# Hybrid two-layer decoder trunk on one core: the last feed-forward slabs regrouped into a fifth pair of seven block products, and the end of each feed-forward phase reordered

## The reference

```python
D_MODEL, SEQ, D_FF, DEPTH = 1024, 512, 2816, 2
DEEPNORM_ALPHA = (2 * DEPTH) ** 0.25
FFN_RES_WEIGHT = 0.5

def swiglu(x, w1, w3, w2):
    return (jax.nn.silu(x @ w1) * (x @ w3)) @ w2

h = swiglu(x, ffn_w1[l, k], ffn_w3[l, k], ffn_w2[l, k])
x = layer_norm(DEEPNORM_ALPHA * x + FFN_RES_WEIGHT * h, ln_g[l, i], ln_b[l, i])
```

## Time and profile before

| what | value |
|---|---|
| median of 3 runs | 1949.17 us (1949.12 to 1950.05) |
| the profiled execution, its own time | 1950.58 us |
| span of its profile | 1948.8 us |
| PE busy | 1928.0 us, 99% of the span, 10793 matmuls |
| DVE, ACT, POOL busy | 1084.5, 633.4, 898.8 us (56, 32, 46%) |
| TensorE clock granted | 0.998 of full over the span |
| DMA | 185.45 MB, mean 95 GB/s |
| chain of work that ended last | PE 97%, DVE 2%, DMA 1% |

### The profile page before, as it was taken

How to read it: one execution, slowest core, us unless ns; L and a number is a source line. 1 busy time by engine, 2 the same in 40 slices (tenths; PEclk the granted TensorE clock), 3 DMA queues, 4 the chain that set the end, 5 groups by cost and what they waited for, 6 DMA issues and landing times.

```text
span 1948.8 us, 26135 instructions
## 1 busy us (share of the span) xinstructions
PE 1928.0 (99%) x10793; PEld 1633.9 (84%) x10793; DVE 1084.5 (56%) x1620; ACT 633.4 (32%) x789; POOL 898.8 (46%) x596
## 2 busy tenths in 40 slices
PE   8999999999999999999999999999999999999997
PEld 8888888978788888888988888889988988888886
DVE  2755473555373665653465647265544675546655
ACT  3333232264423233322333323232233123323321
POOL 4453555533324455445445446444433345355544
PEclk9999999999999999999999999999999999999999
DMA  6232322321204333232423232322222222332321
GB/s 235 92 106 87 130 87 87 106 74 66 66 23 152 109 107 108 65 108 87 152 87 108 65 129 87 108 87 88 69 84 66 66 77 97 108 128 89 108 66 44
DMA packets 135590, 185.45 MB, mean 95 GB/s; under 512 B 3360, under 2 KB 119088, under 8 KB 135472
## 3 DMA queue, kind: packets, MB, share of 16 engines
q1 hardware_dynamic: 135312, 183.53, 28.5%
q10 hardware_dynamic: 160, 0.26, 0.1%
HBM read 181.42 MB, written 2.10 MB: 94 GB/s over the span
## 4 chain that ended last, share of the span: by engine, by line
PE 97%; DVE 2%; DMA 1%; ACT 0%; issue 0%; SPq 0%; POOL 0%; DVEq 0%; ACTq 0%
PE psum L1506 31%; PE psum L1507 30%; PE psum L1508 30%; PE psum L1816 2%; PE psum L1757 1%; PE psum L1530 1%; PE psum L1789 1%; PE psum L1770 1%; DMA raw<-in_ffn_w 1%; PE psum L1844 0%; PE psum L1847 0%; PE psum L1834 0%; DVE xt_lo L1015 0%; DVE arena L1212 0%; ACT w_hi L757 0%
## 5 line engine op out<-in xcount | busy, mean ns | idle before, releaser
L694 POOL TENSOR_TENSOR w_lo<-raw,w_hi 128x512 fp32r<-128x512 f32 x524 | 848.8, 1652 | 922.4 <-ACT w_hi L757 897.8
L1506 PE MATMUL psum<-xt_hi,w_hi 128*128 128x512 f32 (+1 forms) x1824 | 675.0, 370 | 2.2 <-DVE w_lo L1372 0.9
L1507 PE MATMUL psum<-xt_lo,w_hi 128*128 128x512 f32 (+1 forms) x1824 | 670.8, 368 | 0.0
L1508 PE MATMUL psum<-xt_hi,w_lo 128*128 128x512 f32 (+1 forms) x1824 | 670.7, 368 | 0.0
L1506 PEld LDWEIGHTS psum<-xt_hi,w_hi 128*128 128x128 f32 x1824 | 343.8, 188 | 65.3 <-issue 4.5
L1508 PEld LDWEIGHTS psum<-xt_hi,w_lo 128*128 128x128 f32 x1824 | 343.8, 189 | 57.1
L1507 PEld LDWEIGHTS psum<-xt_lo,w_hi 128*128 128x128 f32 x1824 | 343.9, 189 | 55.9
L757 ACT ACTIVATE w_hi<-raw 128x2048 fp32r<-128x2048 f32 x132 | 251.7, 1911 | 345.4 <-PE psum L1508 343.5
L1076 DVE SCALAR_TENSOR_TENSOR x<-psum,x 128x512 f32<-128x512 f32 x224 | 145.6, 684 | 131.5 <-PE psum L1508 128.3
L771 ACT ACTIVATE gate<-psum 128x512 f32<-128x512 f32 x88 | 52.5, 598 | 307.9 <-PE psum L1508 307.9
L1506 PE MATMUL psum<-w_hi,xt_hi 128*128 128x256 f32 (+2 forms) x448 | 139.8, 312 | 0.0
(11 more groups left out here) (178 smaller groups left out, 2147.1 us busy)
## 6 DMA issues: line engine op xcount, KB each, us to landing
raw<-in_ffn_w SPq DMA_DIRECT2D x115, 1024.0 KB, 5.4
raw_odd<-in_ffn_w SPq DMA_DIRECT2D x16, 1024.0 KB, 5.1
raw<-in_hgrn_w_in SPq DMA_DIRECT2D x16, 1024.0 KB, 5.5
raw<-in_attn_w_in SPq DMA_DIRECT2D x9, 1024.0 KB, 6.2
raw<-in_attn_w_out SPq DMA_DIRECT2D x4, 1024.0 KB, 4.9
raw<-in_hgrn_w_out SPq DMA_DIRECT2D x4, 1024.0 KB, 5.0
lng<-in_ln_g SPq DMA_DIRECT2D x6, 512.0 KB, 4.3
lnb<-in_ln_b SPq DMA_DIRECT2D x6, 512.0 KB, 5.4
```

The source lines that it names most:

```text
L694: op = pool.tensor_tensor(w_lo[:, slot_of[s], cols], raw[:, slot_of[s], cols], w_hi[:, slot_of[s], cols].bitcast(F32), ALU.subtract)
L1506: pe.matmul(out_, w[0], xs[0], start=first, stop=False)
L1507: pe.matmul(out_, w[0], xs[1], start=False, stop=False)
L1508: return pe.matmul(out_, w[1], xs[0], start=False, stop=last)
```

## The change

The groups 8 and 9 become a fifth pair (`NP = 5`), so that one down slab, that of group 10, is left. The last pair runs in an order of its own (`LAST_PRODUCTS`), and its last three products P4, P2, P3 stay in their banks: the pieces of the last down slab are accumulated on top of them (`last_down`). x's halves are swapped (`x_piece`), so that the products of one row go to tiles 0 and 1. Of the two kept sums one is left: P1 is added to its quarter and to `kept`, P6 to `kept` (`add_and_keep_first`, `keep_sixth`). The kept sum is added to tiles 0 and 1 after P6, and to tiles 2 and 3 behind the normalisation of tiles 0 and 1. Tile 0 is normalised before tile 1's moments. `turn` uses banks 0 to 3 for tiles 0 and 1 behind an FFN, `begin` has fewer waits there, and GpSimd holds the next phase's second slab back until tile 1 is normalised. The third slab still waits for tile 3. Slots of the ring and the semaphore counts follow. The diff, cut to its core:

```diff
-NP = 4
-UPS = 2 * NG - 1
-FFN_RING = UPS + 4
-SIZES = {"ffn": (FFN_RING, 2, 3), "attn": (13, 4, 4), "hgrn": (20, 4, 4)}
+NP = 5
+UPS = 2 * NG
+FFN_RING = UPS + 1
+SIZES = {"ffn": (FFN_RING, 1, 1), "attn": (13, 4, 4), "hgrn": (20, 4, 4)}
...
+LAST_PRODUCTS = ["P1", "P6", "P5", "P7", "P4", "P2", "P3"]
...
+LAST_ADDED = {"P1": 0, "P6": 4, "P5": 6, "P7": 10}
+N_PAIR_ADDED, N_ADDED = 20, 20 * (NP - 1) + 14
...
+            if p == NP - 1 and name in ("B21", "B22"):
+                k = 2 * (name == "B22")
+                return [part[:, k:k + 2].rearrange("p k j t -> p (k j t)").rearrange("p (c n) -> p c n", c=2)
+                        for part in (a_hi, a_lo)]
...
+        LAST_FFN_BANKS = [bank[i] for i in (2, 0, 3, 1, 4, 6, 5, 7)]
+
+        def turn_bank(turn_no, t):
+
+            return 2 * t if turn_no and phases[turn_no - 1][0] == "ffn" else 4 + 2 * (t % 2)
...
-                            if j == 2:
-                                pool.wait_ge(ln_done, NT * (n + 1))
+                            if j:
+                                pool.wait_ge(ln_done, NT * n + 2 * j)
...
+                    p = NP - 1
+                    high(s0 + UPS - 1)
+                    left_high(fi, p, "A12")
+                    left_high(fi, p, "S1")
+                    left_high(fi, p, "S2")
+                    right_high(n, fi, p, "B11")
+                    left_high(fi, p, "S3")
+                    right_high(n, fi, p, "T2")
                     high(s0 + UPS)
+                    left_high(fi, p, "S4")
+                    left_high(fi, p, "A22")
                     gates(G0 + NG - 1)
-                    high(s0 + UPS + 1)
-                    high(s0 + UPS + 2)
-                    hid_high(hid_odd, G0 + NG - 2, y_done, 8 * (K0 + 1))
-                    high(s0 + UPS + 3)
+                    right_high(n, fi, p, "T1")
+                    right_high(n, fi, p, "T3")
                     for j in range(2):
                         act.wait_ge(hid_done, 2 * (G0 + NG))
                         act.activation(last_h(xt_hi, j), hid[:, j, :].rearrange("p (c n) -> p c n", c=2),
                                        ACT.Copy).then_inc(h_hi_done, 1)
-
+                    right_high(n, fi, p, "T4")
+                    right_high(n, fi, p, "B21")
                     if n < last_phase:
                         high(s0 + FFN_RING)
+                    right_high(n, fi, p, "B22")
+                    if n < last_phase:
                         high(s0 + FFN_RING + 1)
                 else:
...
-                return x[:, 2 * row + t, half * HALF:(half + 1) * HALF]
+                return x[:, 2 * (1 - row) + t, half * HALF:(half + 1) * HALF]
...
+            def keep_tile(f, p, name, t, src, weight):
+
+                if p == 0 and name == "P1":
+                    op = dve.tensor_scalar(kept[:, t, :], src, weight / ALPHA, None, ALU.mult)
+                else:
+                    dve.wait_ge(product_added, kept_at[t])
+                    op = dve.scalar_tensor_tensor(out=kept[:, t, :], in0=src, scalar=weight / ALPHA,
+                                                  in1=kept[:, t, :], op0=ALU.mult, op1=ALU.add)
+                op.then_inc(product_added, 1)
+                kept_at[t] = added_count(f, p, name, 2 * t + 2 if name == "P1" else t + 1)
+
+            def add_and_keep_first(f, p, b0, weight):
 
                 for t in range(2):
-                    dve.wait_ge(product_done, product_count(f, p, name, t))
-                    if p == 0:
-                        op = dve.tensor_scalar(kept[:, t, :], bank[b0 + t][:], weight / ALPHA, None, ALU.mult)
-                    else:
-                        dve.wait_ge(product_added, added_count(f, p - 1, name, t + 1))
-                        op = dve.scalar_tensor_tensor(out=kept[:, t, :], in0=bank[b0 + t][:], scalar=weight / ALPHA,
-                                                      in1=kept[:, t, :], op0=ALU.mult, op1=ALU.add)
-                    op.then_inc(product_added, 1)
+                    dve.wait_ge(product_done, product_count(f, p, "P1", t))
+                    if (0, t, 0) in added_at:
+                        dve.wait_ge(product_added, added_at[0, t, 0])
+                    added_at[0, t, 0] = added_count(f, p, "P1", 2 * t + 1)
+                    dve.scalar_tensor_tensor(out=x_piece(0, t, 0), in0=bank[b0 + t][:], scalar=weight / ALPHA,
+                                             in1=x_piece(0, t, 0), op0=ALU.mult, op1=ALU.add).then_inc(product_added, 1)
+                    keep_tile(f, p, "P1", t, bank[b0 + t][:], weight)
+
+            def keep_sixth(f, p, b0, weight):
+
+                for t in range(2):
+                    dve.wait_ge(product_done, product_count(f, p, "P6", t))
+                    keep_tile(f, p, "P6", t, bank[b0 + t][:], weight)
 
             combined = [0]
...
+            def combine_kept(quarters):
+
                 for t in range(2):
-                    add(kept6[:, t, :], kept1[:, t, :])
-                for t in range(2):
-                    add(x_piece(0, t, 0), kept1[:, t, :])
-                dve.wait_ge(kept_combined, combined[0])
-                for row, half in ((0, 1), (1, 0), (1, 1)):
-                    for t in range(2):
+                    dve.wait_ge(product_added, kept_at[t])
+                    for row, half in quarters:
                         dve.wait_ge(product_added, added_at[row, t, half])
-                        add(x_piece(row, t, half), kept6[:, t, :])
+                        dst = x_piece(row, t, half)
+                        dve.tensor_tensor(dst, dst, kept[:, t, :], ALU.add).then_inc(kept_combined, 1)
...
                 moments(0)
                 add_pieces(1)
+                if gated and n < last_phase:
+                    normalise(0)
                 moments(1)
                 if n == last_phase:
                     dve.wait_ge(par_loaded[0], 16 * (n + 1))
                     centre(0)
                     centre(1)
+                    combine_kept(((0, 1),))
...
-                normalise(0)
+                if not gated:
+                    normalise(0)
                 normalise(1)
-                if phases[n][0] != "ffn":
+                if not gated:
                     add_pieces(2)
                 low_(0)
                 low_(1)
-                if phases[n][0] == "ffn":
+                if gated:
+                    combine_kept(((0, 1),))
                     add_pieces(2)
...
+                    p = NP - 1
+                    hiddens(G0 + 2 * p + 1)
+                    for name in ("S1", "S3", "S2"):
+                        left_sum(fi, p, name)
+                    add_product(fi, p - 1, "P4", 4, [(1, 0)], weight)
+                    left_low(fi, p, "A12")
+                    for name in ("T3", "T2"):
+                        if name == "T2":
+                            right_sum(n, fi, p, "T1")
+                            right_low(n, fi, p, "B11")
+                        right_sum(n, fi, p, name)
+                    left_low(fi, p, "S1")
+                    left_low(fi, p, "S2")
+                    right_low(n, fi, p, "T2")
+                    left_sum(fi, p, "S4")
+                    for name in ("S3", "S4", "A22"):
+                        left_low(fi, p, name)
+                    add_and_keep_first(fi, p, 4, weight)
+                    right_low(n, fi, p, "T1")
+                    dve.wait_ge(right_lo_ready, right_count(fi, p, "T1"))
+                    right_sum(n, fi, p, "T4")
+                    keep_sixth(fi, p, 6, weight)
+                    right_low(n, fi, p, "T3")
+                    combine_kept(((1, 0), (1, 1)))
                     hiddens(G0 + NG - 1)
                     for j in range(2):
-                        dve.wait_ge(h_hi_done, 2 * (H0 + 2) + j + 1)
+                        dve.wait_ge(h_hi_done, 2 * H0 + j + 1)
                         dve.tensor_tensor(last_h(xt_lo, j), hid[:, j, :].rearrange("p (c n) -> p c n", c=2),
                                           last_h(xt_hi, j).bitcast(F32), ALU.subtract).then_inc(h_lo_done, 1)
-                    last_down_and_norm(n, K0 + 1, weight)
+                    right_low(n, fi, p, "T4")
+                    add_product(fi, p, "P5", 4, [(0, 1), (1, 1)], weight)
+                    right_low(n, fi, p, "B21")
+                    add_product(fi, p, "P7", 6, [(1, 0), (1, 1)], weight)
+                    right_low(n, fi, p, "B22")
+                    dve.wait_ge(product_added, N_ADDED * (fi + 1))
+                    last_down_and_norm(n, K0, weight)
...
+            def last_down(s, H, t, half, first):
+
+                if t == 0 and half == 0:
+                    pe.wait_ge(lo_ready, s + 1)
+                    pe.wait_ge(h_lo_done, 2 * H + 2)
+                for c in range(2):
+                    cols = slice(c * D + half * HALF, c * D + (half + 1) * HALF)
+                    mm = three(LAST_FFN_BANKS[2 * t + half][:], left_operand(c, t, True),
```

(22 more changed lines are left out.)

205 lines of the change are left out of this document (69 added, 136 removed).

## The result

The changed kernel takes **1956.51 us** (median of 6 runs, 1952.48 to 1958.05) against 1949.22 of the kernel before: ratio 1.0033, interval 1.0022 to 1.0043. It is slower by 7.3 us; 48 matmuls fewer have bought nothing. The forecast, 1947.4, and its range, up to 1953.5, are both missed. The profiled execution is the shortest of the six, 1952.48 us with a span of 1950.7; the others, up to 5.6 us longer, are explained further down, up to a rest that stays open.

The account below looks back on a forecast made before the run. TensorE was taken as the bound nearly everywhere. Terms: -1.4 us to attention, +1.2 each to FFN and HGRN, -2.6 at the end, together -1.7 on 1949.17, giving 1947.4 us; range 1941.5 to 1953.5.

Parts of the forecast that it names:

- The matmuls (-10.96): Feed-forward phases (FFNs): 48 TensorE matmuls fewer in four FFNs at 0.2285 us each, 10.96 us removed, 2.74 per FFN.
- The walk from h to turn 1 (+1.35 each): FFN end, from h (start of last group's second hidden product): VectorE's chain makes turns 0 and 1 wait, +1.35 us per boundary.
- The kept additions behind turn 1 (+2.55 behind two FFNs, 0 before attention): Two kept-sum adds make tile 3 late for turn 3: +2.55 us before FFN and HGRN, nothing before attention.
- Slack and own length: Behind turn 1: tile 3 has 0.2 us slack against 1.35 of adds; with 0.12 restart, 1.3 us late before port costs.
- The port's share: Kept adds behind turn 1 meeting GpSimd's slab parts: 1.26 us lost, taking VectorE to go first, as at 264.94.
- rival (a): GpSimd goes first at the meeting behind turn 1; each boundary loses 1.2 us more, 1951.1 us; chance 0.16.
- The clock: TensorE's boundary waits were priced with 0.12 us for the first matmul of an emptied array; no clock fall was forecast.
- The last FFN (+0.1): Program's end: VectorE is through by h + 21.5, before the next piece at 21.9; chain keeps its length, +0.1 us.
- (b): Boundaries: VectorE is not held, runs without a pause and keeps GpSimd out; 1942.5 us; chance 0.18.
- (c): Boundaries: everything is covered, the reckoned VectorE chain being 2 or 3 us too long; 1937.8 us; chance 0.08.
- (d): GpSimd's parts hold VectorE from T4 to tile 0's normalisation, 1.26 us per further part per boundary; 1955.0 us; chance 0.10.

Follow-up runs that it names:

- run 8: Changed kernel with all six kept additions done early, plus tile 1's centring split in two halves in the FFNs that are not the last: 1940.86 us, ratio 0.9954.
- Run 4: Changed kernel with TensorE doing unread transposes while it waits ahead of turns 2 and 3 behind an FFN (before attention turn 3 only): 1952.83 us, ratio 1.0014.
- run 5: Kernel before the change, with only two additions of 128x512 put on VectorE ahead of add_pieces(2) behind three FFNs: 1960.71 us, ratio 1.0054.
- run 6: Changed kernel with GpSimd's second slab held until the kept additions are done and, in the last FFN alone, all kept additions early: 1944.61 us, ratio 0.9975.
- runs 1 and 4: The first of the two is the changed kernel again with no edit: 1957.02 us, ratio 1.0034; Run 4 has its own line.
- run 2: Changed kernel with all six kept additions done ahead of the last hiddens, none behind turn 1 or `centre`: 1942.06 us, ratio 0.9960.

## Why the prediction was wrong

**The matmuls (-10.96): held.** 48 records fewer. With the meetings away, the last FFN alone is shorter by 2.65 to 2.7, where the term is 2.74 less 0.1.

**The walk from h to turn 1 (+1.35 each): held, with its two halves wrong.** In the second FFN h is 903.79. T4's low half starts at h + 3.8 (predicted 3.8), B21's at h + 7.3 and is held, 1.65 long, ending at h + 9.0 (9.1); GpSimd's first part started at h + 6.6 (6.7). Tile 0's normalisation starts at h + 16.4 (16.8), which is why turn 0 stands at h + 19.1 and does not wait. Turn 1 comes at h + 23.7 (23.85). So the pair of turns costs 1.2 rather than 1.35, but 1.0 of it is turn 1's, and 0.5 of that is a cause that I had not seen: the power held behind the centring, of which run 8 wins 0.34 back. My own terms, 19.4 + 1.62 + 2.52, put tile 1 at 23.5 and not at the 23.7 that I wrote; with that the term would have been 1.2.

**The kept additions behind turn 1 (+2.55 behind two FFNs, 0 before attention): the step that failed first.** Slack and own length were right: with the port free, turn 3 waits 1.41 (I had 1.3), and before attention nothing. The port's share was taken as 1.26 and is 2.3. That was the choice between the forecast and rival (a), and the row that I leaned on the earlier trace rows does not carry it. The low half at 264.94 had asked 0.06 us before GpSimd's next part, which was held for it:

```profile
265.00 2.31 POOL L694 TENSOR_TENSOR w_lo<-raw,w_hi 128x512 fp32r<-128x512 f32 x1
```

and the next low half, at 266.08, was held for that part in turn. Both went in the order of asking; behind turn 1 it is the part that asks first, if by 0.02 us at most, in all nine meetings. Rival (a) came true, with 3.55 us for the pair in both of the change's profiles. Before attention this leaves 1.16 at turn 3.

**The clock: in no case of mine, and the largest piece.** I priced each wait at its length plus 0.12 for the restart, and so put the clock's part at nothing; it measured 4.2 us. Run 4 shows that, with the same lateness, 4.2 us go when the array is kept busy, and run 5 that a wait of 2.5 us brings the clock down in the old kernel as well. The prediction even had the waits in its text ("2 to 3 us in all at turns 2 and 3"), and did not ask what else hangs on a wait of that length.

**The last FFN (+0.1): wrong in three of the four profiles that have the additions there, and by the times in most runs.** I checked that VectorE has time enough and did not look for who shares the port with the additions there. It is GpSimd's L718, and losing to it costs 2.3 (run 6).

**The sum.** Rival (a)'s 1951.1, with 4.2 for the clock, 2.2 for the last FFN and 0.5 less for turns 0 and 1, is 1957.0; the medians are 1956.5 and 1957.0. The 4.2 is itself a difference between medians (runs 1 and 4), so the test of the rest is run 4: 1951.1 + 2.2 - 0.5 = 1952.8, measured 1952.83. The profiled 1952.48 is the execution in which the clock fell once and VectorE won at the end. What remains open is why the other runs of the change reach 1957 to 1958 where the profiled 1956.04 has both meetings lost and two clock stretches. A third stretch, before attention, would be the right size, but no profile shows it. The mean clocks (0.994, and 0.996 for the profiled one) do not settle it: run 5's profile has three stretches and a mean of 0.996 as well, since the idle tail behind the last matmul is in the mean too.

**Rivals (b) and (c)** fall for the change as it is. But run 2 is (b) nearly to the microsecond (1942.1 against 1942.5), for another reason: the additions are gone from the place, not unheld. **(d)**, the slower one, had the right sign and the wrong place. VectorE is held in the stretch it named by one part, as in my sum, not by three.

**The shared port.** In the nine meetings behind turn 1 the one that starts first, if by 0.02 us or less, has it. But at the handoff in the last FFN GpSimd, asking 0.4 us earlier than the second addition, gets the port in one execution and not in the other. The Trainium skill, SBUF — State Buffer, section Who interferes with whom, says that issue order decides who blocks and, of the two-port modes, that the one that issues first has the shared pair for the whole instruction. Within an instruction the trace agrees (2.89, 1.84, 1.79 us for 0.69). Between instructions of a VectorE that does not pause it doesn't: by that order GpSimd would have won each time. What decides there stays open.

## What to carry to other kernels

Price a new wait of TensorE by its length and by what the clock does behind it: here waits of about 3.5 us in two pieces, or 2.5 in one, cost up to another 1.7 each. When an instruction with two SBUF inputs goes beside GpSimd work, count each at its length plus a whole part of GpSimd, and do not bet on the order. A short instruction of the other engine that someone waits for was served sooner here when the long one was cut in two. And if work has to be done somewhere near a boundary, look for the place with slack ahead of it: the same two additions cost nothing there.
